# Operand chunks of the second MLP product prepared seven ahead of TensorE instead of five

## What is computed

```python
x = layer_norm(ALPHA * x + mx[:, 2] * y_x, ln1_g[l], ln1_b[l])
y_x = sq_relu_mlp(x * (1.0 + mx[:, 4]) + mx[:, 3], w_mlp1[l], w_mlp2[l])
x = layer_norm(ALPHA * x + mx[:, 5] * y_x, ln2_g[l], ln2_b[l])

def sq_relu_mlp(u, w1, w2):
    return jnp.square(jax.nn.relu(u @ w1)) @ w2
```

## Time and profile before

| | us |
|---|---|
| median of 3 runs | 3058.38 |
| lowest and highest run | 3049.83, 3060.05 |
| the profiled execution | 3056.14 |
| its span, first to last instruction | 3054.3 |
| second MLP phase on TensorE, in the span | from 2419.8 |

### The profile page before, as it was taken

How to read it: one execution, slowest core, us unless ns; L and a number is a source line. 1 busy time by engine, 2 the same in 40 slices (tenths; PEclk the granted TensorE clock), 3 DMA queues, 4 the chain that set the end, 5 groups by cost and what they waited for, 6 DMA issues and landing times. The chain is left out here.

```text
span 3054.3 us, 43133 instructions
## 1 busy us (share of the span) xinstructions
PE 2930.5 (96%) x15760; PEld 2200.5 (72%) x15760; DVE 2275.4 (74%) x3182; ACT 1320.1 (43%) x1891; POOL 1382.7 (45%) x833
## 2 busy tenths in 40 slices
PE   5999978999999999999999979999999999999997
PEld 3889855566666566666658858887888888887786
DVE  4445456788887888888778887776777767887788
ACT  3222233444444444444443355555555543443342
POOL 1233324677767867686732243333333144214420
PEclk7999989999999999999999989999999999999999
DMA  6232379524354332434147875447444588787883
GB/s 261 60 88 78 102 229 327 122 73 82 97 119 95 84 78 62 89 75 84 38 141 263 288 293 190 153 153 299 152 152 152 199 317 290 286 312 286 296 296 138
DMA packets 252012, 526.64 MB, mean 172 GB/s; under 512 B 35568, under 2 KB 110832, under 8 KB 240624
## 3 DMA queue, kind: packets, MB, share of 16 engines
q1 hardware_dynamic: 245296, 498.33, 50.6%
q10 hardware_dynamic: 6528, 25.82, 2.1%
HBM read 363.19 MB, written 160.76 MB: 172 GB/s over the span
## 5 line engine op out<-in xcount | busy, mean ns | idle before, releaser
L1340 DVE TENSOR_REDUCE h_mpart<-a_mx 128x1 f32<-128x512 f32 x920 | 537.3, 631 | 154.1 <-PE a_mx L1445 140.7
L1269 POOL TENSOR_TENSOR a_acc_p<-a_acc_p,a_pf 128x1024 f32<-128x1024 f32 x237 | 572.8, 2417 | 152.0 <-ACT a_pf L1320 121.6
L1320 ACT ACTIVATE a_pf<-o_y 128x1024 f32<-128x1024 f32 x432 | 442.1, 1027 | 381.6 <-PE o_y L1492 374.6
L2513 PE MATMUL f_bank<-slots,f_wx 128*128 128x512 f32 x2304 | 534.3, 392 | 14.3 <-DMA slots<-s_uc 8.7
L2521 PE MATMUL f_bank<-slots 128*128 128x512 f32 x2352 | 538.9, 390 | 5.9 <-DVE slots L2292 5.9
L2521 PEld LDWEIGHTS f_bank<-slots 128*128 128x128 f32 x2352 | 442.1, 188 | 99.5 <-DVE slots L2292 7.6
L2513 PEld LDWEIGHTS f_bank<-slots,f_wx 128*128 128x128 f32 x2304 | 436.2, 190 | 107.3 <-DMA slots<-s_uc 10.3
L2459 POOL TENSOR_TENSOR f_work<-raw_rows 128x512 f32<-128x512 f32 x160 | 220.5, 1380 | 381.2 <-DVE f_wx L2285 369.3
L2468 POOL TENSOR_TENSOR f_y<-f_y,raw_rows 128x1024 f32<-128x1024 f32 x72 | 198.4, 2756 | 344.3 <-DMA raw_rows<-in_w 344.3
L2306 DVE TENSOR_TENSOR f_work<-f_work,f_bank 128x512 f32<-128x512 f32 x256 | 174.2, 680 | 135.1 <-ACT f_work L2184 124.3
L553 PE MATMUL p_main<-win_hi,u_hi 128*128 128x512 f32 (+2 forms) x528 | 196.7, 373 | 15.4 <-PEq L75 14.5
(11 more groups left out here) (280 smaller groups left out, 5062.1 us busy)
## 6 DMA issues: line engine op xcount, KB each, us to landing
raw_rows<-s_hx SPq DMA_DIRECT2D x112, 512.0 KB, 4.3
f_y<-in_w SPq DMA_DIRECT2D x104, 512.0 KB, 5.5
raw_rows<-in_w SPq DMA_DIRECT2D x72, 512.0 KB, 6.0
raw_rows<-in_w SPq DMA_DIRECT2D x32, 1024.0 KB, 4.9
s_hx<-stream SPq DMA_DIRECT2D x128, 256.0 KB, 2.7
s_hx<-f_work SPq DMA_DIRECT2D x96, 256.0 KB, 2.0
raw_rows<-in_w_ada SPq DMA_DIRECT2D x8, 2048.0 KB, 8.8
low<-s_mix SPq DMA_DIRECT2D x32, 512.0 KB, 5.4
```

The lines of the kernel that those rows point to most:

```text
L1269: nc.gpsimd.tensor_tensor(acc[:, :], left[:, :], pf[(b * KT + kt) % NPF][:, :], ALU.add).then_inc(added_p, 1)
L1320: nc.scalar.activation(pf[n % NPF][:, :], sc[n % 2][:, :], ACT.Exp, scale=SCALES[0 if is_mla(b) else 1]).then_inc(exped, 1)
L1340: nc.vector.reduce_max(mpart[b % 2][:, s + 4 * half, k:k + 1], bank(("pair", c), half)[:, 0:CHUNKS[k][1]], AX.X).then_inc(mx_read, 1)
L2513: mm = nc.tensor.matmul(by_pair(bank[:, m % 8, :]), w[:, k], x[s][:, :, k * P:(k + 1) * P], start=(k == 0 and j == 0), stop=(k == 3 and j ...
```

## The change

```diff
-        AHEAD, EARLY = 5, 2
+        AHEAD, EARLY = 7, 2
```

## The result

The changed kernel takes 3065.77 us (median of 9 runs, 3062.09 to 3072.97) against 3058.38 before (9 runs, 3049.83 to 3065.57): the ratio is 1.0031, with a 95% interval of 1.0017 to 1.0045. It is slower by some 9.5 us by the ratio (5.2 to 13.8), 7.4 by the medians. Forecast were 3064.8 us and 0.21%.

A forecast was written before the change was run, and what follows sets the result against it. The prediction took VectorE to set the end, with TensorE 7.2 us ahead. Its terms, 7.2 + 0.3 - 2.0 + 0.7 + 0.2, gave +6.4 us on a median of 3058.4: 3064.8 us, 0.21% slower, range 3052 to 3071.

The forecast's parts named there:

- The 8.7 us of TensorE's waits: Second MLP phase: waits for VectorE's low parts, slow clock included, what better supply could give TensorE; counted as 0.
- The waits of ScalarE for TensorE and of TensorE for L2370: Signs in the changed kernel's profile that would prove the forecast wrong: supply tied to TensorE, or TensorE waiting for VectorE's adds.
- neither the slots nor TensorE hold it back: Claim that the supply (load, sum, round, subtract) runs by itself, so a longer reach doesn't speed it up.
- The products 5, 10 and 3: VectorE's adds, eight per product, moving from chunks with a sum to chunks without: +7.2 us and +0.3 us.
- 0.67: Price of a microsecond of VectorE's other work among chunks with a sum, from comparing two such stretches.
- 0.73: Price of a microsecond of VectorE's other work among chunks without a sum, from three such stretches.
- products 4 and 6: VectorE's adds, four per product, moving from chunks without a sum to chunks with: -2.0 us, bounds -4.6 and +0.6.
- product 11 and the last chunks: Four adds moving into the saturated end, +0.7 us; last three chunks now in a row, +0.2 us.
- The stretches without a sum: Three stretches, 25.5, 32.9 and 28.4 us before, each about 1.8 us longer: eight adds come in, four leave.
- the price of 0 under a sum: At their old place the moved adds of products 5 and 10 cost nothing, running while POOL sums and VectorE can't subtract.
- rival B: Moved adds lose all cover, free under sums and full length at the new places: +12.7 us, 3071.1 us; chance 0.25.
- Rival C: The change does nothing that counts, the pattern is shifted and all prices are equal: 3058.4 us; chance 0.23.

## Why the prediction was right

**What bounds the kernel.** That VectorE and its supply set the end, and TensorE has some 7 us in hand, was read from the earlier trace rows and holds: 52 more matmuls cost nothing that was seen, and at three ahead TensorE waits twice as long, which uses up its time in hand but not more. The 8.7 us of TensorE's waits were worth 0, as the sum had it. The waits of ScalarE for TensorE and of TensorE for L2370, which would have shown a bound by slots or banks, aren't in the changed kernel's waits. They aren't absent everywhere, though. In five of the other traces ScalarE waits once or twice for TensorE to free a slot: 0.7 us with the adds back at seven ahead, 1.9 with the adds alone moved, 2.1 at six ahead, 4.8 at four, 2.4 with the adds between. With the adds back it shows so in the waits, and then in the longest piece of the chain that ended last:

```profile
ACT slots L2160 <- PE f_bank L2521: 0.7, 1, 0.7
...
2434.45 196.15 PE f_bank L2521 x864
```

Up to 2631 that execution ran at TensorE's speed. So the prediction's "neither the slots nor TensorE hold it back" is too strong: in the first sum stretch the supply is only just slower than TensorE (170.8 us for 31 chunks, 5.5 for each, where 24 matmuls at 0.224 us make 5.4), and TensorE can set its pace now and then. It doesn't set the end.

**The products 5, 10 and 3**, the terms that made the sum, were forecast at +7.2 and +0.3 us. Moving them alone costs 0.27% (4.6 to 11.9 us, 8.3 in the middle); putting them back saves as much. By the cut adds 12.8 us of them cost 3.4 us at the old place and 9.8 at the new; the forecast's prices give 2.9 (0.67 on product 3's third of it, none on the rest) and 9.3 (0.73 on all).

**The small terms** (products 4 and 6 at -2.0, product 11 and the last chunks at +0.9) can't be told from zero: with the adds back, seven ahead costs 0.04%, and with the adds cut 0.10%, against a forecast of -1.1 us together. Their sign isn't settled. That the sum came within 1 us of the median is in this part luck: by the ratio the loss is 9.5 us, 3.1 more than forecast, and the interval leaves 5.2 to 13.8.

**The stretches without a sum** were forecast 1.8 us longer each. They are 3.4 and 1.6 us longer, and 0.2 us shorter, 4.8 in all against 5.4; the single ones are within what one execution scatters.

**Where the reasoning was thin** is the reason for the price of 0 under a sum. It rested on one piece of one execution, and product 3's adds, which stood between chunks of the same kind, were priced at 0.67 in the same sum. The 0.73 in turn came from `before_ln` pieces, not from adds. In the kernel with the adds back, product 5's adds run between two sums but for the last 0.7 us (DVE, then POOL):

```profile
2703.32 2.47 DVE L2370 TENSOR_TENSOR f_work<-f_work,f_bank 128x512 f32<-128x512 f32 x4
2705.71 1.21 DVE L2290 TENSOR_TENSOR slots<-raw_rows,slots 128x1024 fp32r<-128x1024 f32 x1
2706.85 1.21 DVE L2292 TENSOR_TENSOR slots<-f_y,slots 128x1024 fp32r<-128x1024 f32 x1
2707.98 2.47 DVE L2370 TENSOR_TENSOR f_work<-f_work,f_bank 128x512 f32<-128x512 f32 x4
...
2699.57 2.75 POOL L2468 TENSOR_TENSOR f_y<-f_y,raw_rows 128x1024 f32<-128x1024 f32 x1 [7.89 <-DMA raw_rows<-in_w]
2709.74 2.40 POOL L2468 TENSOR_TENSOR f_y<-f_y,raw_rows 128x1024 f32<-128x1024 f32 x1 [7.43 <-DMA raw_rows<-in_w]
```

The time had come back all the same. And when all adds were put into the wait for a sum, the kernel got slower. So what is shown is that the price goes by place: by the middle values some 0.3 for each us among the last chunks with a sum, 0.6 to 0.8 among those without. Why it is low there is open: that VectorE works under the sum's own time, as I had it, is at most a part; that it waits then anyway for loads that are late (POOL idle for 7.43 us ahead of the sum) would fit both traces and was only argued. The rival B, by which the adds were wholly free at the old place and cost their full length at the new, asked for a loss of 12.7 us, inside the upper end of the interval (13.8). For moving the 24 adds alone it asked for 14.8 us, and that is out: 8.3 (4.6 to 11.9). Which half of it fails isn't shown, since a cost of 0 at the old place (0 to 6.7) and the full one at the new (4.2 to 15.4) are each inside their interval. Rival C, no change, is outside the interval of the change.

## What to carry to other kernels

Read first which engine takes the last result, and how long after TensorE's end; reach or depth that feeds TensorE earns nothing while another engine closes the kernel, until it is so short that the lead is used up, as at three ahead here. A constant that sets how far ahead one kind of work runs also sets where all the other work stands in each engine's order, so cost the neighbours that it moves, by the kind of stretch that they leave and enter. A us of the same work cost less in one place than in the other (by the middle values a third), and idle time that a trace shows isn't free to fill: two kernels that filled it were slower.

## What the runs showed beyond that

Six ahead is slower than five and seven would suggest (1.0036, and 1.0021 with the adds back, where seven with the adds back has 1.0004), so the cost may not be a smooth function of the distance; the intervals leave it open. In the kernel before, all 60 adds of L2370 take 0.67 to 0.68 us from start to end wherever they stand (in a row they start 0.60 us apart), while the subtractions of L2290 and L2292 take 1.2 us or up to 3.4 beside a sum.
